# Two start-up loads of a hybrid decoder trunk issued by ScalarE's queue instead of the sync queue

## The reference, cut to what matters

```python
for l in range(DEPTH):                       # DEPTH = 2, x is 256 x 2048
    h = _rmsnorm(x, ln_g[l])
    u = h @ w_in[l]                          # 2048 x 6232
    ...                                      # GLA, SSD, MLA and dilated attention, gated
    y = jnp.concatenate([y_a, y_b, y_c, y_d], axis=-1)
    x = x + y @ w_out[l]                     # 2048 x 2048
```

## Time and profile before

| what | value |
|---|---|
| median of 3 runs | 820.13 us (819.89 to 820.23) |
| the profiled execution's own time | 820.42 us |
| its span in the profile | 818.6 us |
| PE busy | 812.2 us, 99% of the span |
| DVE, ACT, POOL busy | 606.6, 477.2, 52.8 us |
| read from HBM | 152.32 MB |

### The profile page before, as it was taken

How to read it: one execution, slowest core, us unless ns; L and a number is a source line. 1 busy time by engine, 2 the same in 40 slices (tenths; PEclk the granted TensorE clock), 3 DMA queues, 4 the chain that set the end, 5 groups by cost and what they waited for, 6 DMA issues and landing times.

```text
span 818.6 us, 11315 instructions
## 1 busy us (share of the span) xinstructions
PE 812.2 (99%) x4212; PEld 689.6 (84%) x4212; DVE 606.6 (74%) x1074; ACT 477.2 (58%) x786; POOL 52.8 (6%) x64
## 2 busy tenths in 40 slices
PE   8999999999999999999999999999999999999998
PEld 5888888999888888888888888889998888888886
DVE  6678799877896666678965977979769966665552
ACT  6665544777865576433556465457686575664341
POOL 7100000110200000000000000002012000000000
PEclk9999999999999999999999999999999999999999
DMA  9956544576774757655576655456667546676553
GB/s 329 356 203 204 190 134 155 133 230 169 227 222 155 226 161 231 190 194 180 178 258 180 202 159 178 123 154 185 201 179 229 187 152 206 189 224 214 195 190 118
DMA packets 53367, 159.37 MB, mean 195 GB/s; under 512 B 6144, under 2 KB 10928, under 8 KB 53312
## 3 DMA queue, kind: packets, MB, share of 16 engines
q1 hardware_dynamic: 52800, 158.37, 60.9%
q10 hardware_dynamic: 320, 0.21, 0.1%
q0 software_dynamic: 192, 0.07, 0.1%
HBM read 152.32 MB, written 6.31 MB: 194 GB/s over the span
## 4 chain that ended last, share of the span: by engine, by line
PE 91%; DVE 6%; issue 2%; DMA 1%; SPq 0%; ACT 0%; DVEq 0%
PE gemm L711 27%; PE gemm L702 27%; PE gemm L703 26%; DVE arena L1347 3%; DVE w_lo L1386 2%; PE pairs L885 1%; PE pairs L874 1%; DMA raw<-in_weights_dram 1%; PE pairs L861 1%; PE pairs L866 1%; PE pairs L862 1%; PE pairs L832 1%; PE pairs L768 1%; DVE arena L1470 1%; PE pairs L900 1%
## 5 line engine op out<-in xcount | busy, mean ns | idle before, releaser
L1386 DVE TENSOR_TENSOR w_lo<-raw,w_hi 128x1024 fp32r<-128x1024 f32 (+2 forms) x295 | 324.2, 1108 | 156.8 <-ACT w_hi L1025 155.8
L702 PE MATMUL gemm<-w_hi,a_hi 128*128 128x512 f32 (+1 forms) x1144 | 421.2, 374 | 0.5 <-ACT w_hi L1025 0.5
L703 PE MATMUL gemm<-w_hi,a_lo 128*128 128x512 f32 (+1 forms) x1144 | 414.3, 368 | 0.0
L1025 ACT ACTIVATE w_hi<-raw 128x1024 fp32r<-128x1024 f32 (+2 forms) x295 | 281.6, 967 | 201.9 <-PE gemm L711 141.3
L711 PE MATMUL gemm<-w_lo,a_hi 128*128 128x512 f32 (+1 forms) x1144 | 281.8, 368 | 0.2
L702 PEld LDWEIGHTS gemm<-w_hi,a_hi 128*128 128x128 f32 x1144 | 215.2, 188 | 36.2 <-issue 1.5
L703 PEld LDWEIGHTS gemm<-w_hi,a_lo 128*128 128x128 f32 x1144 | 215.3, 188 | 33.1
L711 PEld LDWEIGHTS gemm<-w_lo,a_hi 128*128 128x128 f32 x1144 | 203.3, 188 | 36.6 <-DVE w_lo L1386 1.9
L610 POOL TENSOR_TENSOR st<-st,powers 128x4 f32<-128x4 f32 (+2 forms) x8 | 8.6, 1075 | 431.2 <-ACT arena L1106 213.9
L1058 ACT ACTIVATE u<-gemm,st 128x512 f32<-128x512 f32 (+1 forms) x40 | 22.1, 605 | 19.3 <-PE gemm L711 19.3
L1221 ACT ACTIVATE arena<-arena,st 128x128 f32<-128x128 f32 (+1 forms) x32 | 13.1, 444 | 31.0 <-DVE st L1663 30.9
(11 more groups left out here) (199 smaller groups left out, 628.4 us busy)
## 6 DMA issues: line engine op xcount, KB each, us to landing
raw<-in_weights_dram SPq DMA_DIRECT2D x225, 512.0 KB, 4.1
raw<-in_weights_dram SPq DMA_DIRECT2D x64, 278.0 KB, 3.0
y_squares<-arena SPq DMA_DIRECT2D x6, 512.0 KB, 5.4
arena<-y_squares SPq DMA_DIRECT2D x24, 128.0 KB, 4.2
raw<-in_weights_dram SPq DMA_DIRECT2D x6, 384.0 KB, 3.5
x<-in_x_dram SPq DMA_DIRECT2D x4, 512.0 KB, 6.2
o<-ssd_rows SPq DMA_DIRECT2D x8, 256.0 KB, 4.7
param_rows<-in_params_dram SPq DMA_DIRECT2D x2, 904.0 KB, 7.8
```

The lines of the kernel that those rows point to most:

```text
L702: pe.matmul(acc_t[t], a_hi[:, k, tok[t]], hi, start=k == 0, stop=False)
L703: pe.matmul(acc_t[t], a_lo[:, k, tok[t]], hi, start=False, stop=False)
L1025: A_(w_hi[:, g % SPLIT, 0:c], raw[:, g % RAW, 0:c], ACT.Copy).then_inc(hi_done, 1)
L1386: TT(w_lo[:, g % SPLIT, 0:c], raw[:, g % RAW, 0:c], w_hi[:, g % SPLIT, 0:c].bitcast(F32), ALU.subtract).then_inc(split_done, 1)
```

## The change

The second half of the first unit and x's k tile 1 are no longer issued by SP. ACT issues both, right behind its load of the column table and ahead of its function table load. The wait for `split_done` stays on SP, and on ACT nothing is waited for ahead of the two. The semaphores and the destinations are the same.

```diff
@@ -520,13 +520,9 @@
             for l in range(DEPTH):
                 for g, n in enumerate(STREAM):
                     sp.wait_ge(split_done, l * PER_LAYER + g + 1)
-                    if (l, n) == (0, 0):
-
-                        sp.dma_start(raw[:, 0, WB:2 * WB], weights(l, n)[:, WB:2 * WB]).then_inc(weights_in[0], 16)
-                    else:
+
+                    if (l, n) != (0, 0):
                         sp.dma_start(raw[:, g % RAW, 0:unit_columns(n)], weights(l, n)).then_inc(weights_in[g % RAW], 16)
-                    if (l, n) == (0, 0):
-                        xT_load(sp, 1)
                     if l == 0 and n < len(XT_PARTS) - 2:
                         xT_load(sp, n + 2)
                     if (l, n) == (0, CONSTS_LOAD):
@@ -986,6 +982,8 @@
             A_ = act_.activation
 
             act_.dma_start(allp[:, :], cols_d).then_inc(cols_in, 16)
+            act_.dma_start(raw[:, 0, WB:2 * WB], weights(0, 0)[:, WB:2 * WB]).then_inc(weights_in[0], 16)
+            xT_load(act_, 1)
             act_.preload_act_table_set("natural_log_exp_and_others")
             act_.wait_ge(cols_in, 16)
 
```

## The result

The changed kernel takes 822.30 us (median of 22 runs, 820.84 to 824.78) against 820.21 of the kernel before (22 runs, 819.66 to 820.57). The ratio is 1.0026 (95% interval 1.0021 to 1.0032): slower by 0.26%, outside the range of 819.2 to 821.3 and on the side that had a chance of 0.08. The spread is as telling as the median: 3.9 us between runs, where the kernel before has 0.9. The profiled execution took 823.16, its span is 821.4.

The account below looks back on a forecast made before the run. PE's matmul stream was taken as the bound, with only unit 1's start movable. Later k tile 1 made ACT ready at 9.96 instead of 9.73: +0.23 us on 820.13, forecast 820.4 us, range 819.2 to 821.3.

Parts of the forecast that it names:

- the side that had a chance of 0.08: Whole kernel: slower by more than 0.2% (1.64 us), given a chance of 0.08.
- What bounds the kernel: Whole span: PE is busy 812.2 of 818.6 us, so only the start of unit 1, at 10.84, matters.
- SP's two issues: SP's queue at the start: two issues fewer save 0.94 us; unit 1's landing moves earlier by 0 to 0.94 us.
- ACT's two issues: ACT before its table load: two added issues take 0.94 us, cost nothing, and leave 0.26 us.
- the cover: ACT before its first copy at 3.66: 1.20 us idle, waiting for the column table, absorbs the added issues.
- k tile 1 changes queues: Loads at the start, the deciding term: k tile 1 lands between 6.90 and 8.38, taken as 7.96, against 7.35.
- The first half now shares: Unit 0's load: first half lands between 4.17 and 7.04, middle 5.6; costs nothing if landed by 5.82.
- The sum: Unit 1's start: ACT ready at 9.96 instead of 9.73, so +0.23 us, giving 820.4 us, forecast as no change.
- 2.00 us of work on ACT: ACT between k tile 1's landing and unit 1's copy: 2.00 us, added to 7.96 to give 9.96.
- The slower rival: Start of unit 0: first half lands only with the second, at 7.04; 821.5 to 824.5 us, chance 0.15.
- the second price: PE's unit 0 matmuls: after idling from 5.2 to nearly 8, slow pace costs 1.5 to 3.0 us more at most.
- The gain rival: Start of unit 1: k tile 1 lands at 6.90, unit 1 moves by up to 0.83 us; 819.3 to 819.6, chance 0.33.

Follow-up runs that it names:

- the first experiment: The changed kernel with k tile 1 back on SP's queue, only the second half of unit 0 on ACT's: 820.28 us, ratio 0.9999 to the kernel before.

## Why the prediction was wrong, point by point

- **What bounds the kernel**: right. Only the start moved, and PE has no new wait behind it.
- **SP's two issues**: done as said, unit 1 issued at 2.11. The bound was not: unit 1's data was to land between 8.79 and 9.73 and landed at 10.3. "The number of bytes in front of unit 1's end is the same" left out that bytes of pieces issued behind it can move first.
- **ACT's two issues**: right. The table load began at 2.14, the first copy at 3.67, with 0.25 us of the cover left (0.26 forecast).
- **k tile 1 changes queues**: this step failed. Its latest landing was set at 8.38, the moment when the bytes of k tiles 2 and 3 and all ahead had come before, and 0.42 us were taken off for idle engine time. It came at 9.24. The bound took it that only three transfers on each queue share the engines until k tile 1 is in. In fact pieces issued later were moving beside it: in the queue counts from 8 to 9 us, when k tile 1 was still not all in, SP's queue (q1) moved 0.38 MB and ACT's (q10) its last 0.01 MB:

```profile
q1 hardware_dynamic: 101, 0.38, 96.2%
q0 software_dynamic: 8, 0.01, 2.3%
q10 hardware_dynamic: 7, 0.01, 1.6%
```

  The two halves, k tiles 0 to 3, the column table and POOL's transfers are 1.14 MB together. When k tiles 2 and 3 landed, at 9.04, the engines had moved 2.05 MB (9.04 us at 227 GB/s), so 0.91 MB of later pieces, more than the whole of unit 1 (0.52), had gone in between. In the kernel before it was 1.73 MB by 8.38 (207 GB/s), 0.59 of it later pieces. So "the bytes of all have come" was no bound: in the kernel before, too, later pieces had gone in between. The windows up to these two moments, of the kernel before and of the changed kernel:

```profile
0.00:8.38 8.38, 6.04 (x10) 2.54 (x10) 2.05 (x4) 3.45 (x5) 3.72 (x15) 1.00 0.72 207
```

```profile
0.00:9.04 9.04, 5.39 (x10) 2.14 (x10) 1.57 (x3) 2.42 (x3) 2.44 (x11) 1.00 0.72 227
```

  With SP's later transfers withheld k tile 1 came at 6.62; with k tile 1 back on SP's queue it came at 6.21. The total rate was no worse: adding the windows from 2 to 9 us, the engines moved 2.01 MB, against 1.97 before. The same bytes came in a worse order.
- **The first half now shares**: right. It landed at 4.87, between 4.17 and 7.04 and short of the 5.82 up to which it costs nothing, and it cost nothing in the median of the first experiment. What the sum left out is the gap that it opens in PE ahead of unit 0 (0.68 us), behind which some executions may lose pace ("The clock" above).
- **The sum**: +0.23 us was forecast, +2.09 measured. With k tile 1 at 9.24, my own steps give PE's second half 1.17 us behind it, at 10.41, exactly as seen, and by PE's path +1.42 for unit 1. The rest is the clock, for which the sum had no term. One more term was off: the "2.00 us of work on ACT" between k tile 1 and unit 1's copy took 1.74 (9.24 to 10.98). In the kernel before the copies of k tiles 2 and 3 began 0.68 us behind that of the second half (7.76, 8.44), here 0.52 (9.66, 10.18); those pieces had landed only at 8.38, so a wait for them was counted as work.
- **The slower rival** named the second price, and in the profiled execution its place was another. It let PE idle in front of the first half (5.2 to nearly 8) and lose pace there; PE idled there for only 0.68 us and kept its pace, then idled between the halves (7.99 to 10.41) and lost it. For the eight runs above 822 with a mean clock of 1.000 the rival's place is still open. I had two bounds for k tile 1 and priced only its landing; that a longer idle stretch there could bring the clock down, I asked only of the other stretch. The 1.0 us of idle time in the kernel before, with full pace behind it, said nothing of 2.4.
- **The gain rival**: its condition, k tile 1 at 6.90 from ACT's queue, was not met. With k tile 1 kept on SP's queue something of it may be there (three variants near 819.5), within what can hardly be told.
- **The Trainium skill's rule** ("DMA: Bandwidth & Descriptors", section "Issuing engines are not separate DMA queues"), that several issuing engines save only issue time, is borne out as the upper bound that I used it for: the 0.94 us of issue time came off and reached nothing. The loss came from the order that the one queue had kept, 1.9 us of k tile 1's landing. The same page's rule of whole packets (section "Queues, rings and completion order") would have put the first half at 4.17 or at 7.04; the halves landed 0.2 us apart, at 4.87 and 5.08, which is neither. Whether the turns were shorter than a packet, or the 16 engines took the halves in different orders, no view here tells.

## What to carry to other kernels

One queue that issues in the order of need was a schedule here, if a loose one; moving a transfer to a second queue took it out of that order, and what the first queue issued next shared the engines with it. Before such a move, ask of the moved transfer not when it is issued but what will be moving beside it until its last row has come, and put on the second queue only what is in nobody's way when late or what is first there. Price every idle stretch of PE twice: once for its length and once for the clock that it may lose.

## What the runs showed of the hardware that was not expected

- A transfer can be delayed by those behind it on its own queue: k tiles 2 and 3 took 7.4 us with unit 1 and more behind them, and 4.8 us when SP held those back. (With POOL's transfers late they took 5.7, so those have a part in the 7.4.) Why the last rows of a transfer come so late is not settled here.
- PE's granted clock in the windows reads 1.00 at the very start, where matmuls still run at the lower pace. With SP holding back, PE's matmuls from 7.45 to 10.01 us start 0.43 us apart and are of the long kind (0.63 us, as the one at 7.88 above), and the window says

```profile
7.00:8.00 1.00, 1.00 (x3) 0.81 (x4) 0.80 (x2) 1.00 (x4) 0.87 (x2) 1.00 0.42 74
```

  From 10.38 on they start 0.23 us apart, and the column still says 1.00. So until the pace has first risen the column, and the mean made of it, say nothing of the pace; the length of the records does.
- One program (the changed kernel with the short matmul) took 820.1 to 825.2 us in its runs, with a mean granted clock of 1.000 to 0.995. In these runs a change that left PE idle for 2 to 3 us at the start made the kernel unsteady as well as slow.
